# Reordering one gated-delta turn: which projections stand beside which step, and where ScalarE and VectorE take the next pair's convolutions and the old pair's gating

## The chip, the cores and the metric

The kernel runs on one core of a Trainium2 chip. The metric is the time of the whole program on the device in microseconds (us), lower is better. TensorE (PE) multiplies, VectorE (DVE), ScalarE (ACT) and GpSimd (POOL) do the rest, SyncE (SP) issues the loads. Each engine works through its own instructions in order and waits on semaphores for the others.

## The reference

Two blocks in a row over a sequence of 512 tokens of width 1024 in float32. The first has four SwiGLU feed-forward layers, a gated linear attention and a sparse attention. The second has a gated delta rule mixer and a forgetting attention, each behind a modulated norm. The change touches the gated delta mixer alone:

```python
def gated_delta_rule(q, k, v, g, beta):
    ...
    L = jnp.where(strict, jnp.einsum('bhncd,bhnsd->bhncs', kb, k) * decay, 0.0)
    T = lax.linalg.triangular_solve(eye + L, jnp.broadcast_to(eye, L.shape),
                                    left_side=True, lower=True, unit_diagonal=True)
    u = T @ vb
    w = T @ (kb * jnp.exp(g)[..., None])
    attn = jnp.einsum('bhncd,bhnsd->bhncs', q, k) * decay
    ...
    def step(state, inp):
        v_new = u_n - jnp.einsum('bhcd,bhde->bhce', w_n, state)
        o = (jnp.einsum('bhcd,bhde->bhce', q_n, state)
             + jnp.einsum('bhcs,bhse->bhce', a_n, v_new))
        state = state * gl_n[..., None, None] + jnp.einsum('bhcd,bhce->bhde', k_n, v_new)
        return state, o

def gdn_mixer(h, w_in, conv_w, A_log, dt_bias, norm_w, w_out):
    ...
    proj = h @ w_in
    ...
    qkv = jax.nn.silu(causal_depthwise_conv(qkv, conv_w))
    ...
    o = gated_delta_rule(q, k, v, g, beta)
    zg = jax.nn.silu(z.reshape(B, S, GDN_V_HEADS, GDN_HEAD_DIM).astype(jnp.float32))
    o = rmsnorm(o, norm_w) * zg
    return o.reshape(B, S, GDN_V_WIDTH).astype(h.dtype) @ w_out
```

Between the convolution and the rule q and k are normalised per head; each of the 8 q/k heads serves 2 of the 16 v heads.

## The kernel before, in words

Large products are made in split precision: a weight block of 128 x 1024 is loaded into `w_raw`, ScalarE rounds it to `w_hi` (L237), VectorE makes the rest `w_lo` (L243), and TensorE multiplies three times, hi by hi, hi by lo, lo by hi (L255). There are four raw and four split buffers, and splits run three blocks ahead of the products.

The gated-delta stage goes through 8 turns (`gdn_turns`): "first", six "mid" (a hardware loop of three rounds with two turns in its body), and "last". A turn j treats one q/k head with its two v heads. At the same time it projects q, k, v0, v1 of pair j+1 and z of pair j, and it makes the output tiles O0 to O7 of pair p = j-1. Each projection is cut into four units of six matmuls ("v12" is unit 2 of v1), and an output tile is one unit of six matmuls (L1749 to L1751). Results stand in a ring of four PSUM banks. The chain of a turn itself is made of small products: transposes "kt", "vt", the products "kk" and "qk", "sel" (L1816, picks rows for 15 elimination steps that VectorE makes on 16 x 16 blocks), then products of 64 x 64 (L1718), "f", "g", "c", "f2", "v", "y", "at", each of which combines blocks of the inverse, and then four chunks t of the recurrence: "ks" (L1848), "vn" (L1853), "o" (L1862, L1864), "ds" (L1867). At the end the squares of the output are summed (L1871).

What order stands where is written out by hand, engine by engine:

- TensorE: the table `GDN_BESIDE` names for each step the units that follow it. In a middle turn "v11 v12" stand beside "v", "v13 O0" beside "y", O1 beside "at", and "z11 z12 z13" beside "o3". Beside "at" also come the sums of the next pair's squares (`sums_next`, L1760), which read the buffers `G.sq`.
- ScalarE (`gdn_act`, `turn`): copies of small products ("fa", "fb", "c", "f2a", "y", "bt", "ct", all at L1996), splits (`GDN_SPLITS`), for the next pair the first tap of each convolution (`conv`, L1908), its silu (`silu`, L1913), the squares of q and k (`squares`, L1920) and copies of their sums (`sums`, L1925); for the old pair the high part of the gated output (`high`, L1989).
- VectorE (`gdn_dve`, `turn`): elimination steps, copies "ga", "gb", "f2b", "at", additions "va", "vb", the other three taps of each convolution (`conv`, L2112), for the old pair the product with the gate (`gated`, L2158), the low part (`low`, L2163) and the addition of output tiles into the residual (L2121).

`G.sq` is used twice: it holds the old pair's output until `low` has read it, and then the squares of the next pair. So `squares` waits for "lo_1". `silu(u)` waits until VectorE has done the last tap of convolution u (it frees the bank). TensorE's "at" waits for ScalarE's "bt", an output tile 0 for "lo_1".

## Time and profile before

| | |
|---|---|
| median of 3 runs | 2972.32 us (2971.85 to 2976.83) |
| the profiled execution | 2976.83 us, its span 2975.1 us |
| PE busy | 2822.0 us, 95% |
| DVE busy | 1664.2 us, 56% |
| ACT busy | 1249.0 us, 42% |
| POOL busy | 621.2 us, 21% |
| gated-delta turns (2025 to 2520) | about 71 us each |
| last chain, by engine | PE 77%, DVE 9%, ACT 5% |

The timeline gives one line for each instruction or run of equal ones: its start in us from the start of the span, its length, engine, line of the kernel, operation and tiles, the count (x), and in brackets the idle time of the engine just before it with what ended it. Matmuls overlap, so a row lasts longer than its distance to the next: 0.39 us long, 0.23 us apart for 512 columns at the full clock. Products of 64 x 64 and of 128 columns are made in several passes, so one step gives many counts.

### The profile page before, as it was taken

What the parts mean: (1) busy time and instruction counts of PE and PEld (TensorE: products, weight loads), DVE (VectorE), ACT (ScalarE), POOL (GpSimd) and SP (SyncE); (2) the same over time, 40 slices, a digit from 0 to 9 for tenths busy, and PEclk for the clock granted to TensorE, in tenths of its full rate; (3) what the DMA queues carried; (4) which work ended last, traced back from release to release, by engine and by line L of the source; (5) the groups of instructions that cost most, each with busy time, mean ns of one, the idle gap of its engine ahead of it and who ended that gap; (6) DMA issues with size and microseconds to landing.
All of it is one profiled execution on the core that took longest, in us unless ns stands there. A gap on an engine that the chain in (4) does not pass through costs nothing.

```text
span 2975.1 us, 41230 instructions
## 1 busy us (share of the span) xinstructions
PE 2822.0 (95%) x14333; PEld 2280.8 (77%) x14333; DVE 1664.2 (56%) x2500; ACT 1249.0 (42%) x1838; POOL 621.2 (21%) x594
## 2 busy tenths in 40 slices
PE   7999999999998999999898999979999999789998
PEld 5888877788887788886677788857888887567766
DVE  4444345454433664336845654265777777677773
ACT  4443242444423332233443322254555554456664
POOL 2000003100001440013424500214333333112221
PEclk8999998999999999999899999989999999899999
DMA  4333331233333553332114533312222222122211
GB/s 121 104 98 95 91 91 52 70 106 92 97 97 88 170 169 97 95 88 71 43 57 140 170 113 96 92 41 81 69 66 65 65 65 54 36 64 57 56 57 57
DMA packets 485304, 255.64 MB, mean 86 GB/s; under 512 B 18820, under 2 KB 479399, under 8 KB 485175
## 3 DMA queue, kind: packets, MB, share of 16 engines
q1 hardware_dynamic: 483856, 253.25, 29.8%
q8 instruction: 80, 1.31, 0.2%
q10 hardware_dynamic: 1318, 0.69, 0.1%
q14 instruction: 50, 0.40, 0.0%
HBM read 251.77 MB, written 2.13 MB: 85 GB/s over the span
## 4 chain that ended last, share of the span: by engine, by line
PE 77%; DVE 9%; ACT 5%; issue 4%; POOL 4%; ACTq 0%; DMA 0%; DVEq 0%; POOLq 0%; SPq 0%
PE bank L255 60%; PE bank L1718 2%; ACT w_hi L237 1%; POOL sumsq L585 1%; PE bank L2569 1%; POOL ada_sum L585 1%; DVE dsa_work L1456 1%; PE bank L1749 1%; PE bank L1816 1%; PE bank L1750 1%; PE bank L1751 1%; DVE prod L681 1%; DVE w_lo L243 1%; DVE small L1454 1%; DVE ada_hi L571 1%
## 5 line engine op out<-in xcount | busy, mean ns | idle before, releaser
L255 PE MATMUL bank<-x_hi,w_hi 128*128 128x512 f32 x2328 | 957.9, 411 | 10.0 <-DVE x_lo L484 3.5
L255 PE MATMUL bank<-x_hi,w_lo 128*128 128x512 f32 x2328 | 916.5, 394 | 0.0
L255 PE MATMUL bank<-x_lo,w_hi 128*128 128x512 f32 x2328 | 916.3, 394 | 0.0
L243 DVE TENSOR_TENSOR w_lo<-w_raw,w_hi 128x1024 fp32r<-128x1024 f32 x430 | 551.0, 1283 | 639.6 <-ACT w_hi L237 632.8
L237 ACT ACTIVATE w_hi<-w_raw 128x1024 fp32r<-128x1024 f32 x430 | 451.1, 1053 | 447.8 <-PE bank L255 414.2
L255 PEld LDWEIGHTS bank<-x_hi,w_hi 128*128 128x128 f32 x2328 | 442.8, 190 | 119.6 <-issue 19.9
L255 PEld LDWEIGHTS bank<-x_hi,w_lo 128*128 128x128 f32 x2328 | 442.1, 190 | 95.9
L255 PEld LDWEIGHTS bank<-x_lo,w_hi 128*128 128x128 f32 x2328 | 443.7, 191 | 91.9 <-issue 7.4
L400 POOL TENSOR_TENSOR sumsq<-sumsq,sq 128x512 f32<-128x512 f32 x54 | 91.6, 1697 | 1351.1 <-ACT sq L386 1349.7
L255 PE MATMUL bank<-h_hi,w_hi 128*128 128x512 f32 x832 | 323.9, 389 | 4.0 <-DVE h_lo L2675 2.4
L255 PE MATMUL bank<-h_hi,w_lo 128*128 128x512 f32 x832 | 323.7, 389 | 0.0
L255 PE MATMUL bank<-h_lo,w_hi 128*128 128x512 f32 x832 | 323.7, 389 | 0.0
L657 ACT ACTIVATE h_hi<-prod 128x512 f32 x88 | 55.6, 632 | 403.1 <-DVE prod L681 403.1
L255 PEld LDWEIGHTS bank<-h_hi,w_hi 128*128 128x128 f32 x832 | 156.2, 188 | 36.6 <-issue 4.3
L255 PEld LDWEIGHTS bank<-h_lo,w_hi 128*128 128x128 f32 x832 | 156.2, 188 | 32.6
L255 PEld LDWEIGHTS bank<-h_hi,w_lo 128*128 128x128 f32 x832 | 156.2, 188 | 32.3
L654 ACT ACTIVATE gate_s<-gate_s 128x512 f32<-128x512 f32 x88 | 55.6, 632 | 192.4 <-DVE gate_s L673 192.4
L678 DVE TENSOR_TENSOR prod<-bank,rstd 128x512 f32<-128x512 f32 x88 | 60.6, 689 | 101.8 <-PE bank L255 101.8
L684 DVE TENSOR_TENSOR h_lo<-prod,h_hi 128x512 f32 x88 | 62.2, 706 | 82.3 <-ACT h_hi L657 82.3
L585 POOL TENSOR_TENSOR sumsq<-sumsq,ada_hi 128x512 f32<-128x512 f32 x48 | 62.0, 1292 | 164.1 <-DVE ada_hi L571 164.1
L673 DVE TENSOR_TENSOR gate_s<-bank,rstd 128x512 f32<-128x512 f32 x88 | 60.4, 687 | 37.7 <-PE bank L255 37.7
L681 DVE TENSOR_TENSOR prod<-prod,gate_s 128x512 f32<-128x512 f32 x88 | 76.6, 871 | 4.5
(446 smaller groups left out, 3590.1 us busy)
## 6 DMA issues: line engine op xcount, KB each, us to landing
w_raw<-in_ffn_wi_dram SPq DMA_DIRECT2D x176, 512.0 KB, 3.8
w_raw<-in_ffn_wo_dram SPq DMA_DIRECT2D x64, 512.0 KB, 4.0
w_raw<-in_ada_w_dram SPq DMA_DIRECT2D x48, 512.0 KB, 4.9
w_raw<-in_a_w_in_dram SPq DMA_DIRECT2D x48, 512.0 KB, 4.0
w_raw<-in_b_w_in_dram SPq DMA_DIRECT2D x32, 512.0 KB, 4.1
w_raw<-in_ffn_wo_dram SPq DMA_DIRECT2D x32, 384.0 KB, 3.5
w_raw<-in_even_w_in_dram SPq DMA_DIRECT2D x16, 512.0 KB, 4.1
w_raw<-in_a_w_out_dram SPq DMA_DIRECT2D x16, 512.0 KB, 3.6
```

The lines of the kernel that those rows point to most:

```text
L237: act.activation(w_hi[b % SPLIT][:], w_raw[raw % RAW][:], ACT.Copy).then_inc(w_hi_done, 1)
L243: dve.tensor_tensor(w_lo[s][:], w_raw[raw_of(b) % RAW][:], w_hi[s][:].bitcast(F32), ALU.subtract).then_inc(w_lo_done, 1)
L255: mm = pe.matmul(out, lhs[:, w], rhs(kt), start=first and kk == 0 and m == 0, stop=last and kk == len(kts) - 1 and m == 2)
L400: pool.tensor_tensor(sumsq[:], sumsq[:], sq[k % 2][:], ALU.add).then_inc(sum_added, 1)
L585: pool.tensor_tensor(dst, x, y, ALU.add).then_inc(ada_added, 1)
L654: act.activation(gate_s[s][:], gate_s[s][:], ACT.Silu).then_inc(silu_done, 1)
L657: act.activation(h_hi[:, col(i * 2 + 2 * turn0 + s)], prod[s][:], ACT.Copy).then_inc(h_hi_done, 1)
L673: dve.tensor_tensor(gate_s[s][:], bank[(t0 + o) % BANKS][:], rstd[:], ALU.mult).then_inc(tile_free, 1)
L678: dve.tensor_tensor(prod[s][:], bank[(t0 + o + 1) % BANKS][:], rstd[:], ALU.mult).then_inc(tile_free, 1)
L681: dve.tensor_tensor(prod[s][:], prod[s][:], gate_s[s][:], ALU.mult).then_inc(prod_done, 1)
L684: dve.tensor_tensor(h_lo[:, h], prod[s][:], h_hi[:, h].bitcast(F32), ALU.subtract).then_inc(h_ready, 1)
L1718: mm = pe.matmul(out[:, c * INV_PART:(c + 1) * INV_PART], lhs(c), rhs(c), start=True, stop=True)
```

## The change

Nothing is computed otherwise; instructions change places on three engines.

TensorE, middle turn: "v12" moves from beside "v" to "y", "v13" from "y" to "at", O0 to beside "vn0" and each later output tile behind it by one or two steps, so that five units of z instead of three stand beside "o3". First and last turn are shifted likewise (in the last, nothing stands beside "v" and O0 stands beside "y").

ScalarE: silu of k moves from behind the copies "y" and "bt" to before the old pair's high parts, and so before these copies; the first tap of v0 from before the high parts to behind the squares; the first tap of v1 behind the copies of the sums.

VectorE: the gating of the old pair moves from before "ga" to behind the additions "va", "vb"; the low parts from before "va" to behind the copy "at" (in the last turn before it); the split "f" from behind the convolution of k to before it; the convolutions of v0 and v1 both behind the split "f2"; output tiles are added one or two steps later.

ScalarE in the middle turn before, from behind the copy of f2 (`gdn_W_0_231`); `gdn_kT_207` is k and `gdn_vT_234` is v0 of the next pair, `gdn_W_0_229` and `gdn_T` are the targets of copies "y" and "bt":

```order
L1996 ACTIVATE gdn_W_0_231<-bank 64x512
L1907 REGISTER_ALU
L1908 ISA
L1908 ACTIVATE gdn_vT_234<-bank,par 128x512
L1988 REGISTER_ALU
L1989 ACTIVATE gdn_o_hi_190<-gdn_sq_200 128x512
L1988 REGISTER_ALU
L1989 ACTIVATE gdn_o_hi_191<-gdn_sq_201 128x512
L237 ACTIVATE w_hi_58<-w_raw_54 128x1024
L1992 REGISTER_ALU
L1996 ACTIVATE gdn_W_0_229<-bank 64x512
L1996 ACTIVATE gdn_T<-bank 64x8x64
```

The same place of ScalarE now:

```order
L1994 ACTIVATE gdn_W_0_231<-bank 64x512
L236 REGISTER_ALU
L237 ACTIVATE w_hi_58<-w_raw_54 128x1024
L1912 REGISTER_ALU
L1913 ACTIVATE gdn_kT_207<-gdn_kT_207 128x512
L1986 REGISTER_ALU
L1987 ACTIVATE gdn_o_hi_190<-gdn_sq_200 128x512
L1986 REGISTER_ALU
L1987 ACTIVATE gdn_o_hi_191<-gdn_sq_201 128x512
L1990 REGISTER_ALU
L1994 ACTIVATE gdn_W_0_229<-bank 64x512
L1994 ACTIVATE gdn_T<-bank 64x8x64
```

The silu of k stands ahead of the two copies now, the tap of v0 has left this place, and the split has moved up.

VectorE in the middle turn before, from the split "vc" to the convolution of k; `gdn_W_1_232` is the target of the additions "va", "vb", and `gdn_sq` holds the old pair's gated output:

```order
L243 TENSOR_TENSOR w_lo_60<-w_raw_52,w_hi_56 128x1024
L2162 REGISTER_ALU
L2163 TENSOR_TENSOR gdn_o_lo_192<-gdn_sq_200,gdn_o_hi_190 128x512
L2162 REGISTER_ALU
L2163 TENSOR_TENSOR gdn_o_lo_193<-gdn_sq_201,gdn_o_hi_191 128x512
L2166 REGISTER_ALU x2
L2173 TENSOR_TENSOR gdn_W_1_232<-gdn_W_1_230,bank 64x512 x2
L2106 REGISTER_ALU
L2107 REGISTER_ALU
L2112 ISA
L2112 SCALAR_TENSOR_TENSOR gdn_kT_207<-bank,par,gdn_kT_207 128x511
```

The same place of VectorE now, from the additions on:

```order
L2173 TENSOR_TENSOR gdn_W_1_232<-gdn_W_1_230,bank 64x512 x2
L2156 REGISTER_ALU
L2157 REGISTER_ALU
L2158 TENSOR_TENSOR gdn_sq_200<-gdn_sq_200,gdn_zs_211 128x512
L2156 REGISTER_ALU
L2158 TENSOR_TENSOR gdn_sq_201<-gdn_sq_201,gdn_zs_212 128x512
L241 REGISTER_ALU
L243 TENSOR_TENSOR w_lo_61<-w_raw_53,w_hi_57 128x1024
L2107 REGISTER_ALU
L2112 ISA
L2112 SCALAR_TENSOR_TENSOR gdn_kT_207<-bank,par,gdn_kT_207 128x511
```

The gating and a split stand between the additions and the convolution of k. The low parts have moved on, to behind the copy "at", which writes `gdn_T`:

```order
L2112 SCALAR_TENSOR_TENSOR gdn_kT_207<-bank,par,gdn_kT_207 128x509
L2166 REGISTER_ALU
L2254 COPY gdn_T<-bank 64x8x64
L2162 REGISTER_ALU
L2163 TENSOR_TENSOR gdn_o_lo_192<-gdn_sq_200,gdn_o_hi_190 128x512
L2162 REGISTER_ALU
L2163 TENSOR_TENSOR gdn_o_lo_193<-gdn_sq_201,gdn_o_hi_191 128x512
L241 REGISTER_ALU
L243 TENSOR_TENSOR w_lo_62<-w_raw_54,w_hi_58 128x1024
```

Behind them now stand a split and the convolutions of v0 and v1.

The diff, with the table cut to the middle turn and without the order of semaphore names:

```diff
--- before.py
+++ after.py
@@ -1581,13 +1581,13 @@
 
 
         GDN_BESIDE = {
...
-            "mid": {"kt": "q0", "kk": "q1", "vt": "q2", "sel": "q3", "inv": "k0 k1 k2 k3 v00 v01 v02", "c": "v03", "f2": "v10", "v": "v11 v12", "y": "v13 O0",
-                    "at": "O1", "vn0": "O2", "ds0": "O3", "ks1": "O4", "vn1": "O5", "ds1": "O6", "ks2": "O7", "vn2": "z00", "ds2": "z01",
-                    "ks3": "z02", "vn3": "z03 z10", "o3": "z11 z12 z13"},
+            "mid": {"kt": "q0", "kk": "q1", "vt": "q2", "sel": "q3", "inv": "k0 k1 k2 k3 v00 v01 v02", "c": "v03", "f2": "v10", "v": "v11", "y": "v12",
+                    "at": "v13", "vn0": "O0", "ds0": "O1", "ks1": "O2", "vn1": "O3", "ds1": "O4", "ks2": "O5", "vn2": "O6", "ds2": "O7",
+                    "ks3": "z00", "vn3": "z01 z02", "o3": "z03 z10 z11 z12 z13"},
...
         GDN_SPLITS = {"first": {"start": "q", "vc": "k", "f": "v0", "f2": "v1", "at": "z0", "end": "z1"},
                       "mid": {"start": "q", "vc": "k", "f": "v0", "f2": "v1", "at": "Oa", "vn3": "Ob", "end": "z0 z1"},
...
@@ -1912,9 +1912,7 @@
                 act.wait_ge(*at.taken(GDN_CONV[u], i))
                 act.activation(x[:], x[:], ACT.Silu).then_inc(*N.act.done(f"cs{u}"))
 
-            def squares(j, odd, p=None):
-                if p is not None:
-                    act.wait_ge(*GdnOut.dve.after("lo_1", p))
+            def squares(j, odd):
                 for u in range(2):
                     act.wait_ge(*N.act.after(f"cs{u}", j))
                     act.activation(G.sq[u][:], gdn_conv(u, odd)[:], ACT.Square).then_inc(*N.act.done(f"sq_{'qk'[u]}"))
@@ -1955,12 +1953,12 @@
             act.wait_ge(*G.prep_dve.after("diff"))
             act.activation(G.kd, G.diff, ACT.Exp).then_inc(*s.done("kd"))
             silu(0, 0, front, 0)
+            silu(1, 0, front, 0)
             split(front, 0, "v0")
+            squares(0, 0)
             conv(2, 0, 0, front, 0)
-            silu(1, 0, front, 0)
-            squares(0, 0)
+            sums(0)
             conv(3, 0, 0, front, 0)
-            sums(0)
             split(front, 0, "v1")
             for u in (2, 3):
                 silu(u, 0, front, 0)
@@ -2028,18 +2026,19 @@
                     silu(0, i, at, odd)
                 pe("f2")
                 run("f2a", G.F2[a, :], first(0)[a], ACT.Copy)
+                splits("f2")
                 if more:
-                    conv(2, j + 1, i, at, odd)
+                    silu(1, i, at, odd)
                 if p is not None:
                     high(p)
-                splits("f2")
                 pe("y")
                 run("y", G.CY[b, :], first(0)[b], ACT.Copy)
                 run("bt", G.T[b, :, b], halves(first(1)[b]), ACT.Copy)
                 if more:
-                    silu(1, i, at, odd)
-                    squares(j + 1, odd, p)
-                    conv(3, j + 1, i, at, odd)
+                    if p is not None:
+                        act.wait_ge(*GdnOut.dve.after("lo_1", p))
+                    squares(j + 1, odd)
+                    conv(2, j + 1, i, at, odd)
                 else:
                     for h in range(2):
                         gate(h, at.through(f"z{h}", i), at.bank(f"z{h}"), (tile_free, BANKS + at.tile[f"z{h}"]))
@@ -2049,6 +2048,7 @@
                     sums(j + 1)
                 splits("at")
                 if more:
+                    conv(3, j + 1, i, at, odd)
                     silu(2, i, at, odd)
                 for t in range(TT):
                     for h in range(2):
@@ -2231,8 +2231,6 @@
                     if p is not None:
                         dve.wait_ge(*gdn_gate(at, i, 1)[3])
                     conv(0, j + 1, i, at, odd)
-                if p is not None:
-                    gated(p, [gdn_gate(at, i, h)[3] for h in range(2)])
                 pe("g")
                 for n, r, src in (("ga", a, second(0)), ("gb", b, second(1))):
                     dve.tensor_copy(G.m[r, :], src[r]).then_inc(*done(n))
@@ -2241,23 +2239,26 @@
                 pe("f2")
                 dve.tensor_copy(G.F2[b, :], first(1)[b]).then_inc(*done("f2b"))
                 splits("vc")
-                if p is not None:
-                    low(p)
                 pe("v")
                 own("hb")
                 for n, r, src in (("va", a, second(0)), ("vb", b, second(1))):
                     tt(n, G.V[r, :], G.V1[r, :], src[r], ALU.add)
+                if p is not None:
+                    gated(p, [gdn_gate(at, i, h)[3] for h in range(2)])
+                splits("f")
                 if more:
                     conv(1, j + 1, i, at, odd)
-                splits("f")
+                else:
+                    low(p)
+                pe("at")
+                dve.tensor_copy(G.T[a, :, a], halves(first(0)[a])).then_inc(*done("at"))
+                if more and p is not None:
+                    low(p)
+                splits("f2")
                 if more:
                     conv(2, j + 1, i, at, odd)
-                pe("at")
-                dve.tensor_copy(G.T[a, :, a], halves(first(0)[a])).then_inc(*done("at"))
-                if more:
                     conv(3, j + 1, i, at, odd)
-                splits("f2")
-                if not more and p is not None:
+                elif p is not None:
                     dve.wait_ge(tile_free, BANKS + at.tile["O0"])
                     outs(0, 1)
                 splits("at")
@@ -2269,7 +2270,7 @@
                             dve.scalar_tensor_tensor(G.W1[h][:, 3 * P:4 * P], first(h)[:, 3 * P:4 * P], G.neg_eg[:, bass.ds((j * 2 + h) * TT + t, 1)],
                                                      G.v_tok[h][:, x], ALU.mult, ALU.add).then_inc(*done(f"r{t}_{h}"))
                     if more:
-                        outs(*((0,), (2,), (5,), (7,))[t])
+                        outs(*((), (1, 2), (4,), (7,))[t])
                     else:
                         outs(*((2,), (3,), (5,), (7,))[t])
                     for h in range(2):
@@ -2283,7 +2284,7 @@
                         else:
                             dve.tensor_copy(S, add).then_inc(*done(f"s{t}_{h}"))
                     if more:
-                        outs(*((1,), (3, 4), (6,), ())[t])
+                        outs(*((0,), (3,), (5, 6), ())[t])
                     else:
                         outs(*((), (4,), (6,), ())[t])
                     splits(f"vn{t}")
```

## Rows read from the trace of the kernel before

**Rows 1.** The page, part 1: busy time, share of the span and count of instructions of each engine.

```profile
PE 2822.0 (95%) x14333; PEld 2280.8 (77%) x14333; DVE 1664.2 (56%) x2500; ACT 1249.0 (42%) x1838; POOL 621.2 (21%) x594
```

**Rows 2.** Stretches: length; busy us (instructions) of PE, PEld, DVE, ACT, POOL; TensorE's granted clock; DMA; GB/s.

```profile
2172.00:2243.00 71.00, 69.51 (x518) 56.95 (x517) 51.40 (x94) 37.20 (x61) 22.84 (x17) 1.00 0.24 69
```

**Rows 3.** Timeline of TensorE in a middle turn.

```profile
2176.90 1.15 PE L1718 MATMUL bank<-gdn_W,gdn_W 64*64 64x64 f32 x32
2177.97 0.50 PE L255 MATMUL bank<-x_hi,w_hi 128*128 128x512 f32 x1
...
2180.92 0.27 PE L1718 MATMUL bank<-gdn_W,gdn_W 64*64 64x64 f32 x1
...
2184.95 0.27 PE L1718 MATMUL bank<-gdn_P,gdn_W 64*64 64x64 f32 x1
...
2187.52 1.88 PE L1760 MATMUL bank<-gdn_sq,ones 128*128 128x512 f32 x4
2189.24 0.61 PE L1853 MATMUL bank<-gdn_v_tok,gdn_T 128*128 128x128 f32 x4
...
2190.84 0.40 PE L1751 MATMUL bank<-gdn_o_hi,w_lo 128*128 128x512 f32 x1
2191.81 0.49 PE L1864 MATMUL bank<-gdn_attnT,gdn_W 128*128 128x128 f32 x2 [0.57 <-ACT gdn_W L1996]
```

**Rows 4.** Waits of the stage, 2000 to 2600: us in total, times, longest.

```profile
PE bank L1816 <- DVE gdn_blocks L2195: 6.1, 6, 2.0
```

**Rows 5.** Timeline of VectorE in the same turn.

```profile
2171.47 1.28 DVE L2158 TENSOR_TENSOR gdn_sq<-gdn_sq,gdn_zs 128x512 f32<-128x512 f32 x2
...
2177.29 1.29 DVE L2163 TENSOR_TENSOR gdn_o_lo<-gdn_sq,gdn_o_hi 128x512 fp32r<-128x512 f32 x2
2178.61 1.40 DVE L2173 TENSOR_TENSOR gdn_W<-gdn_W,bank 64x512 f32<-64x512 f32 x2
2180.05 2.54 DVE L2112 SCALAR_TENSOR_TENSOR gdn_kT<-bank,par,gdn_kT 128x511 f32<-128x511 f32 x3
2182.50 1.30 DVE L243 TENSOR_TENSOR w_lo<-w_raw,w_hi 128x1024 fp32r<-128x1024 f32 x1
2183.72 2.52 DVE L2112 SCALAR_TENSOR_TENSOR gdn_vT<-bank,par,gdn_vT 128x511 f32<-128x511 f32 x3
2186.16 0.67 DVE L2256 COPY gdn_T<-bank 64x512 f32<-64x512 f32 x1
```

**Rows 6.** Timeline of ScalarE in the same turn.

```profile
2176.47 1.14 ACT L1989 ACTIVATE gdn_o_hi<-gdn_sq 128x512 fp32r<-128x512 f32 x2
2177.51 1.05 ACT L237 ACTIVATE w_hi<-w_raw 128x1024 fp32r<-128x1024 f32 x1
2182.11 0.60 ACT L1996 ACTIVATE gdn_W<-bank 64x512 f32<-64x512 f32 x1 [3.55 <-PE bank L1718]
2182.61 0.58 ACT L1996 ACTIVATE gdn_T<-bank 64x512 f32<-64x512 f32 x1
2183.22 0.63 ACT L1913 ACTIVATE gdn_kT<-gdn_kT 128x512 f32<-128x512 f32 x1
2183.75 0.62 ACT L1920 ACTIVATE gdn_sq<-gdn_qT 128x512 f32<-128x512 f32 x1
...
2189.93 1.05 ACT L237 ACTIVATE w_hi<-w_raw 128x1024 fp32r<-128x1024 f32 x1
```

**Rows 7.** Timeline of TensorE, the first middle turn's start and the last turn.

```profile
2076.57 1.15 PE L1708 MATMUL bank<-gdn_kT 128*128 128x128 f32 x8 [2.47 <-ACT gdn_W L1976]
...
2079.86 0.63 PE L255 MATMUL bank<-x_hi,w_lo 128*128 128x512 f32 x1
...
2514.68 2.03 PE L1816 MATMUL bank<-gdn_blocks,sumsq 128*128 128x128 f32 x8 [2.02 <-DVE gdn_blocks L2195]
...
2559.64 1.98 PE L1871 MATMUL bank<-gdn_W,ones 128*128 128x512 f32 x4 [0.76 <-ACT gdn_W L1996]
```

**Rows 8.** Stretches of TensorE: length, busy us (instructions), granted clock, DMA, GB/s.

```profile
2076.00:2080.00 4.00, 3.43 (x19) 0.73 0.50 135
```

## What the change was predicted to do

> **What bounds the kernel now.** I read the page's engine line first, then the table of stretches for the gated-delta stage, then the timelines of TensorE, VectorE and ScalarE through one middle turn, then the waits. TensorE is busy 95% of the span [rows 1], and in a middle turn of this stage 69.51 us of 71 at full clock [rows 2]. So a turn can gain only what TensorE still waits, and it loses every microsecond that another engine comes late. Two waits of a middle turn are marked. The product of L1864 starts 0.97 us after the last matmul before it, where 0.23 is the pace, so it waits 0.74 us for ScalarE. The product of L1816 waits for VectorE's reductions, six times in the stage, 6.1 us in all [rows 3, 4]. A third wait is unmarked: f2 is about 0.17 us late because VectorE gates the old pair's rows before it copies "gb".
>
> Between "v" and "at" the three engines run close together. "v" starts at 2176.90, two units (12 matmuls, 1.37 us a unit) cover VectorE's additions, "y" starts at 2180.92, two more units cover ScalarE's copies "y" and "bt", and "at" starts at 2184.95 [rows 3]. ScalarE is idle for 3.55 us before copy "y", so it is early. VectorE's rows from 2177.29 on carry no idle time, so it is the one that runs without a rest there [rows 5, 6].
>
> **The change, part by part.** All times are for the middle turn shown. Up to f2 nothing moves but the gating (1.20 us from one instruction to the next), so f2 and "v" start about 0.17 us earlier, "v" at 2176.73.
>
> *v to y.* VectorE's additions start at 2177.95 and end at 2179.35 (1.40) [rows 5]. One unit instead of two stands beside them on TensorE, so "y" could start at 2179.41 and starts at about 2179.50. Wait: 0.1.
>
> *y to at, the main term.* "at" needs ScalarE's copy "bt". With one unit beside "y" TensorE is ready at 2182.18. But ScalarE's silu of k now stands ahead of copies "y" and "bt", and it waits for VectorE's convolution of k. VectorE does, from 2177.95 on: additions 1.44, gating 1.20, weight split 1.22, convolution 2.45 (distances from start to start in [rows 5]; neither the gating nor the split stood between them before). The convolution ends at 2184.26. Then ScalarE: silu 0.53, the two high parts 1.04, "y" 0.50, "bt" 0.58 [rows 6], which ends at 2186.98; "at" starts at 2187.1. Wait: 4.9 us. ScalarE's early split of the weights costs nothing, it fits into the idle time.
>
> *at to sums.* The low parts now stand behind VectorE's copy of "at". That copy comes 1.21 us after "at" starts, 2188.3, and takes 0.63; the low parts end 1.32 later, 2190.25. Only then may ScalarE overwrite the two buffers with squares, 0.53 for the first. The sums of L1760 start at about 2191.0. TensorE, with one unit beside "at", is ready 2.57 us after "at" (2184.95 to 2187.52 in [rows 3]), at 2189.67. Wait: 1.35.
>
> *sums to vn0's copies.* The sums take 1.72, so ScalarE's second copy of them can start at 2192.9. Behind it stand a split (1.05 long, 0.95 to the next), now also the first tap of v1's convolution (0.6), the silu of v0 (0.5) and then the copies that L1864 needs, which it sees 0.4 after their start [rows 3, 6]. L1864 starts at 2195.87; TensorE, after the sums, vn0 (0.36) and one unit, is ready at 2194.43. Wait: 1.45, where 0.74 stood.
>
> *The first state copy.* VectorE still owes after the low parts: split 1.22, convolution of v0 2.45 (from 2192.1, when ScalarE has laid its first tap), that of v1 2.5 (from 2195.05, likewise), split 1.22. Its state copies start at 2198.7, and L1848 at 2199.0. TensorE is ready at 2198.2. Wait: 0.85. From here on the turn runs as before; output tiles come one or two steps later, and each bank is freed in time. The splits that moved also release SyncE's loads (a raw buffer is free after its low split); the last of them comes about 8 us later, and its buffer is read again only in the next turn, so I cost that at nothing; a load that came late would show as ScalarE waiting for DMA.
>
> *The turn's end.* Five units of z stand after the last L1864 instead of three. ScalarE, GpSimd and VectorE, whose chain leads from there to L1816, get 2.74 us more cover. But the sums of L1871 come later too, and with them ScalarE's roots and VectorE's split, so VectorE's reductions come about 1.5 later. Net cover is 1.2, more than the 0.8 to 1.0 that is waited. This wait goes: -0.98 in five middle turns. What is late next there is f, which has 0.6 in hand.
>
> A middle turn thus waits 0.1 + 4.9 + 1.35 + 1.45 + 0.85 = 8.65 and loses 0.17 + 0.74 of old waits: +7.74. Six of them: +46.4; L1816 in five of them: -4.9.
>
> *First turn.* No old pair, so no gating, no high and low parts: 4.9 less 1.20, 1.04 and some tenths is 2.5; the sums wait for nothing, the later two waits stay. +4.0.
>
> *Last turn.* The first output tile waits for the low parts, which come 1.20 + 1.22 + 1.32 = 3.7 after VectorE's additions while TensorE has only "y" to do: 2.7 waited, and "y" itself waits 0.9 more, since nothing stands beside "v". Against it stand the 2.02 that L1816 waits there (of which its later reductions, 1.2 as above, give only 1.5 back) and 0.76 at the last sums [rows 7]. Net 2.7 + 0.9 - 1.5 - 0.8 = +1.3. *Before the first turn* the squares pass one tap (-0.5 at best), but the tap of v1 now waits for the copies of the sums, and VectorE and the roots follow it by an instruction's length: +0.6, the later end.
>
> Sum without the clock: 46.4 - 4.9 + 4.0 + 1.3 + 0.6 = +47.4 us.
>
> *The clock.* After a wait of 2.47 us before L1708 the matmuls of the next microseconds took 0.63 instead of 0.39, and the granted clock of that stretch is 0.73, so both levels, 2.4 and 1.2 GHz, lie in it; after the wait of 2.02, eight products of L1816 took 2.03 instead of 1.13, and the waits under 1 us were followed by no such row [rows 3, 7, 8]. Each fall cost about 1.6 us of dense work. A wait of 4.9 will do the same in each turn. But behind "at" TensorE waits again for the others, so part of the slow work is hidden: bounds 0 and 3.3 (two falls), I take 0.8, half of one fall, near the lower end because the row nearest to it has dense work behind it and this place has not. Six times: +5.
> The Trainium skill ("TensorE: Matmul & The Clock Gate", "HAM oscillation — how this bites in real kernels") says that idle gaps between bursts of matmuls put the array back to half rate at every gap. It speaks against this change; by it each turn pays a fall, by the rows under 1 us no turn paid one before. The trace agrees with both halves.
>
> The profiled execution took 2976.83 us with a span of 2975.1; the median of the three runs is 2972.32, the low one 2971.85, so the profiled one is the slowest by 4.5. The sum goes on the median: 2972.3 + 52.4 = 3024.7, say 3025.
>
> **The rivals.** (A) *The clock falls deeper.* Two falls in each middle turn, for "at" and for L1864, with little hidden: 47.4 + 6 x 3.3 = +67, 3039. For it: the wait is twice as long as any that the rows show inside the loop, and three others follow within 12 us. Against: those others are under 1.5. The page named above would give this, if every gap counted.
> (B) *The later waits melt.* VectorE and ScalarE catch up while TensorE waits for "at", so only that wait counts: 6 x (4.9 + 0.1) - 6 x 0.17 - 4.9 + 2.5 + 1.3 + 0.6 = +28.5, 3001. Against it: VectorE's debt behind "at" (low parts, two splits, two convolutions, 8.7 us) can't be worked off earlier, since it stands behind the copy of "at" in its order.
> (C) *Faster.* Only the turns' ends and f2 count: -4.9, -1.5 - 0.8 in the last turn, -6 x 0.17, together -8.2, 2964. It needs the convolution of k to end 4.9 us earlier than I have it, before 2179.4; from that point silu, high parts and copies are hidden under the unit of "y". For it: the wait at L1816 is real and its cover is. Against: additions, gating, split and convolution are 6.3 us in one row on one engine, behind "v".
> (D) *No change:* the middle wait is about 1 us and eats the gain of the end. It needs 3.9 us of slack that no row shows.
>
> **How the numbers follow.** My forecast 0.62, (A) 0.18, (B) 0.13, (C) 0.04, (D) 0.03. The forecast's own range is 3014 to 3034: clock 0 to one whole fall in each turn, and 0.7 us for a turn's waits. With (A) whole and (B) as far as 3007, the range is 3006 to 3044. A measurement of this kernel tells 0.2% (6 us) from no change. Slower by more than that: forecast, A and B, 0.93; within: D, 0.03; faster: C, 0.04.
>
> **What would show it.** In the changed kernel's timeline of a middle turn: ScalarE's silu of gdn_kT starts right behind VectorE's third convolution step, with ScalarE idle 4 to 7 us before it; L1718's last group ("at") shows TensorE idle near 4.9 us, for ScalarE; L1760 waits for a square, 1 to 1.5 us; L1864 waits 1.2 to 1.7; the wait of L1816 is gone in the middle turns; rows of 0.63 us instead of 0.39 stand behind "at"; the stretch that a turn fills grows from 71 or 72 us to 78 to 80. I am wrong if TensorE's idle time before "at" is under 2 us, if the later waits are nearly nothing (B), or if L1816 still waits.

## The result, and the profile after

The changed kernel takes 3046.21 us (median of 4 runs, 3043.9 to 3049.34); the kernel before takes 2972.09 us beside it. The ratio is 1.0247, interval 1.0229 to 1.0265: **slower**, as forecast, but by 74 us where the forecast's sum said 52.4, and 2 us above the end of the range (3044). The profiled execution took 3047.69 us with a span of 3045.9, 70.8 us more than the span before; the accounts below are made on these two spans.

The first line of the page, the stretch of 71 us that holds most of the middle turn, and the 5 us behind "at" (columns as in [rows 2]):

```profile
PE 2839.6 (93%) x14333; PEld 2291.7 (75%) x14333; DVE 1675.4 (55%) x2500; ACT 1250.6 (41%) x1838; POOL 626.9 (21%) x594
```

```profile
2184.00:2255.00 71.00, 61.74 (x473) 49.52 (x472) 43.83 (x60) 33.82 (x56) 23.71 (x17) 0.93 0.25 68
2204.50:2209.50 5.00, 4.95 (x39) 3.88 (x40) 2.95 (x4) 0.94 (x2) 0.00 (x0) 0.50 0.01 3
```

The same number of instructions on every engine; TensorE is busy 61.74 us of 71 where it was 69.51 [rows 1, 2], and the granted clock of the last line is 0.50, the 1.2 GHz level, over the whole 5 us. The waits of TensorE in the stage, 2000 to 2680 (line waited at and what ended the wait; us in total, times, longest):

```profile
PE bank L1718 <- ACT gdn_T L1994: 45.5, 7, 7.2
PE bank L1730 <- POOL gdn_kT L2324: 10.1, 1, 10.1
...
PE bank L1864 <- ACT gdn_W L1994: 8.2, 7, 1.3
PE bank L1848 <- DVE gdn_W L2285: 4.6, 8, 0.7
PE bank L1718 <- DVE gdn_W L2173: 2.8, 7, 1.6
```

The wait before "at" stands at the top, with 7.1 to 7.2 us in each middle turn and 2.6 in the first. L1816, which led to 6.1 us before [rows 4], is gone from the list. TensorE's timeline of a middle turn, to be laid beside [rows 3]:

```profile
2194.68 0.24 PE L1718 MATMUL bank<-gdn_W,gdn_W 64*64 64x64 f32 x1 [0.23 <-DVE gdn_W L2173]
...
2204.55 0.34 PE L1718 MATMUL bank<-gdn_P,gdn_W 64*64 64x64 f32 x1 [7.13 <-ACT gdn_T L1994]
...
2207.04 0.63 PE L255 MATMUL bank<-x_lo,w_hi 128*128 128x512 f32 x1
...
2209.25 2.42 PE L1760 MATMUL bank<-gdn_sq,ones 128*128 128x512 f32 x4
2211.51 0.61 PE L1853 MATMUL bank<-gdn_v_tok,gdn_T 128*128 128x128 f32 x4
...
2214.66 0.49 PE L1864 MATMUL bank<-gdn_attnT,gdn_W 128*128 128x128 f32 x2 [1.15 <-ACT gdn_W L1994]
```

and VectorE's, ScalarE's and GpSimd's of the same place, to be laid beside [rows 5, 6]:

```profile
2193.01 1.40 DVE L2173 TENSOR_TENSOR gdn_W<-gdn_W,bank 64x512 f32<-64x512 f32 x2 [0.81 <-PE bank L1718]
2194.44 2.37 DVE L2158 TENSOR_TENSOR gdn_sq<-gdn_sq,gdn_zs 128x512 f32<-128x512 f32 x2
2196.74 2.30 DVE L243 TENSOR_TENSOR w_lo<-w_raw,w_hi 128x1024 fp32r<-128x1024 f32 x1
2199.07 2.54 DVE L2112 SCALAR_TENSOR_TENSOR gdn_kT<-bank,par,gdn_kT 128x511 f32<-128x511 f32 x3
2206.55 0.68 DVE L2254 COPY gdn_T<-bank 64x512 f32<-64x512 f32 x1 [4.95 <-PE bank L1718]
...
2201.63 0.63 ACT L1913 ACTIVATE gdn_kT<-gdn_kT 128x512 f32<-128x512 f32 x1 [9.84 <-DVE gdn_kT L2112]
...
2203.82 0.58 ACT L1994 ACTIVATE gdn_T<-bank 64x512 f32<-64x512 f32 x1
...
2194.59 3.36 POOL L2317 TENSOR_TENSOR gdn_dec<-gdn_gb,not_above 128x512 f32<-128x512 f32 x2 [22.58 <-DVE gdn_W L2173]
2197.91 3.02 POOL L2320 TENSOR_TENSOR gdn_dec<-gdn_dec,gdn_cols 128x512 f32<-128x512 f32 x2
```

The path of the forecast is there link by link: additions, gating, split, convolution of k, then ScalarE's silu of k at the moment the convolution ends, the high parts, the two copies, "at". But two links are longer than they were: the gating 2.37 instead of 1.28 and the split 2.30 instead of 1.30 [rows 5]. They lie exactly beside GpSimd's L2317 and L2320. GpSimd is released by VectorE's additions ("vb"), which stood ahead of the convolution before and stand ahead of the gating and the split now.

Where the 70.8 us of span are, by the starts of "f" (32 small products of L1718) in both traces: from the first middle turn on, five periods take 71.64 us each before (2098.11 to 2456.31) and 82.17 after (2102.18 to 2513.04), and the sixth, up to the last turn's "f", 71.40 and 80.55. That is 5 x 10.53 + 9.15 = 61.8 us. The last turn gives 4.85 from "f" to L1871 (31.93 to 36.78), the first 4.7 from "f" to "f" (65.95 to 70.67), and the front of the stage, from the products of L1777 to the first "f", 0.5. Ahead of that, where the kernels are the same, the changed one is 1.1 early in its trace (L1777 at 1982.30 instead of 1983.43). Together 70.7. Below, "us a turn" is always the mean of such periods without the sixth. Where a run is set against the changed kernel in us of the whole time, it goes by the two ratios, since each stands against its own runs of the kernel before.

### The profile page after: what moved, and what is told of

Read it like the earlier page. It is cut to its first block, busy times and chain, and to the rows that moved or that the text cites. A ratio compares the mean times of both kernels' runs of the same rounds, so it can differ in the third digit from the quotient of the medians.

```text
span 3045.9 us, 41218 instructions
## 1 busy us (share of the span) xinstructions
PE 2839.6 (93%) x14333; PEld 2291.7 (75%) x14333; DVE 1675.4 (55%) x2500; ACT 1250.6 (41%) x1838; POOL 626.9 (21%) x594
## 3 DMA queue, kind: packets, MB, share of 16 engines
q8 instruction: 80, 1.31, 0.2%
HBM read 251.77 MB, written 2.13 MB: 83 GB/s over the span
## 4 chain that ended last, share of the span: by engine, by line
PE 75%; DVE 11%; ACT 5%; issue 4%; POOL 3%; ACTq 0%; DMA 0%; DVEq 0%; POOLq 0%; SPq 0%
PE bank L255 59%; PE bank L1718 2%; DVE w_lo L243 1%; ACT w_hi L237 1%; POOL sumsq L585 1%; PE bank L2570 1%; POOL ada_sum L585 1%; DVE dsa_work L1456 1%; DVE prod L681 1%; DVE small L1454 1%; PE bank L1816 1%; PE bank L1749 1%; PE bank L1751 1%; PE bank L1750 1%; DVE ada_hi L571 1%
## 5 line engine op out<-in xcount | busy, mean ns | idle before, releaser
L243 DVE TENSOR_TENSOR w_lo<-w_raw,w_hi 128x1024 fp32r<-128x1024 f32 x430 | 553.0, 1287 | 646.0 <-ACT w_hi L237 639.2
```

The costliest lines, as they stand in the source:

```text
L243: dve.tensor_tensor(w_lo[s][:], w_raw[raw_of(b) % RAW][:], w_hi[s][:].bitcast(F32), ALU.subtract).then_inc(w_lo_done, 1)
```

## The experiments

Three theories of the 21 us that the forecast missed. **Contention:** VectorE's gating and split, both with two operands in SBUF, are held up by GpSimd's two pairs of products, some 2.3 us a turn. **Clock:** the half clock behind the long wait costs more than the 0.8 us counted. **Order:** the chain is longer than counted through its order alone (table, place of the silu, place of the low parts). They exclude one another only in size, so each was taken out by itself, and at the end the first two together.

### GpSimd released later

```diff
-                    dve("PT" if p is None else "vb")
+                    dve("PT" if p is None else "s0_1")
```

> The changed kernel, but GpSimd begins its additions for the next pair's decay behind VectorE's second state copy of chunk 0 instead of behind the addition vb. Theory 1 (VectorE's gating and split run at half speed because GpSimd's tensor operations run beside them): the gating takes 1.28 us again (2.37 in the changed kernel) and the split beside it 1.23 to 1.30 (2.30), TensorE's wait before at falls from 7.1 to about 4.9, six middle turns give 6 x 2.2 = 13 us: 3033. Rival (the excess over the forecast is the clock's): both stay near 2.3 and the time stays within 3 us of 3046.

Measured 3039.52 us, ratio 1.0208 (1.0189 to 1.0226), 79.88 us a turn. VectorE in the same place:

```profile
2191.81 1.29 DVE L2158 TENSOR_TENSOR gdn_sq<-gdn_sq,gdn_zs 128x512 f32<-128x512 f32 x2
2193.02 1.22 DVE L243 TENSOR_TENSOR w_lo<-w_raw,w_hi 128x1024 fp32r<-128x1024 f32 x1
```

and the first line of TensorE's waits, 2000 to 2600:

```profile
PE bank L1718 <- ACT gdn_T L1994: 32.6, 7, 5.0
```

Gating and split are back at the durations of [rows 5] with VectorE's own order unchanged, and the wait falls from 7.2 to 5.0, next to the 4.9 forecast. A turn saves 82.17 - 79.88 = 2.29 us, and VectorE's busy time is 1662.6 us instead of 1675.4. Contention is shown.

### GpSimd released after the copy of "at"

The same line, with "at" in place of "s0_1".

> The changed kernel, but GpSimd begins behind VectorE's copy of at. Theory 1: gating 1.28 and split 1.30 as above, the wait before at 4.9, but now the low parts (1.28) and the split behind them (1.21) run beside GpSimd and take 2.3 to 2.4 each; the low parts lie on the path to the sums, the split is hidden by VectorE's wait for the tap of v0. Net 2.2 - 1.1 = 1.1 a turn, 3039. Rival (something else slows gating and split in their new place): they stay at 2.3, the low parts at 1.28, 3046.

Measured 3038.03 us, 1.0209 (1.019 to 1.0228), 79.75 us a turn. The time is near the 3039 expected, but not for its reason. Which engine is held up was expected wrongly:

```profile
2200.96 1.28 DVE L2163 TENSOR_TENSOR gdn_o_lo<-gdn_sq,gdn_o_hi 128x512 fp32r<-128x512 f32 x2
2202.16 1.21 DVE L243 TENSOR_TENSOR w_lo<-w_raw,w_hi 128x1024 fp32r<-128x1024 f32 x1
...
2201.21 4.52 POOL L2317 TENSOR_TENSOR gdn_dec<-gdn_gb,not_above 128x512 f32<-128x512 f32 x2 [33.26 <-DVE gdn_T L2254]
```

VectorE's low parts and split keep their 1.28 and 1.21, and GpSimd's pair takes 4.52 us, where it took 2.54 with GpSimd released after the state copy. VectorE was at it first, and GpSimd's first product came through only when VectorE's row of such instructions was over. Nothing waits for GpSimd there, so it costs nothing.

### The kernel before, GpSimd released earlier

```diff
-                    dve("PT" if p is None else "vb")
+                    dve("PT")
```

> The kernel before with one edit on GpSimd: its part of each turn for the next pair (L2317, L2320 and on) is released after VectorE's copy PT in every turn instead of after the additions in the later turns, so it starts some 10 us earlier and runs beside VectorE's gating (L2158). Theory (VectorE's products of two SBUF operands and GpSimd's delay each other when they run side by side, and nothing in the changed kernel's order is needed for that): the rows of L2158 or L243 that fall beside GpSimd's L2317 and L2320 take 2.2 to 2.4 us instead of 1.3, rows that read PSUM (L2112, L2173) stay at 2.54 and 1.40; TensorE loses at most 1.2 us a turn at f2 or v: ratio 1.000 to 1.003. Rival (the slow gating of the changed kernel comes from its own operands or place in the order): all rows of L2158 and L243 stay at 1.3 us.

Measured 2983.2 us beside 2978.09 for before, ratio 1.0016 (1.0006 to 1.0025); 72.61 us a turn. VectorE's gating in the old order, GpSimd beside it, and TensorE's "g", which VectorE's next copies release:

```profile
2172.51 2.35 DVE L2158 TENSOR_TENSOR gdn_sq<-gdn_sq,gdn_zs 128x512 f32<-128x512 f32 x2
...
2172.83 2.93 POOL L2319 TENSOR_TENSOR gdn_dec<-gdn_dec,gdn_cols 128x512 f32<-128x512 f32 x2
...
2176.33 1.15 PE L1718 MATMUL bank<-gdn_W,gdn_W 64*64 64x64 f32 x32 [1.16 <-DVE gdn_W L2238]
```

The contention can be made at will without any of the change's moves: 2.35 us for the gating, and 1.0 us a turn on TensorE.

### The silu of k back behind the copies

ScalarE's `silu(1)` back from ahead of the high parts to behind "bt"; all else as in the changed kernel:

```diff
-                if more:
-                    silu(1, i, at, odd)
                 if p is not None:
                     high(p)
                 pe("y")
...
                 if more:
+                    silu(1, i, at, odd)
                     if p is not None:
                         act.wait_ge(*GdnOut.dve.after("lo_1", p))
```

> The changed kernel with ScalarE's silu of k put back behind the copies y and bt, all else as changed. If the wait before at comes from that silu: at waits about 1.8 (for the high parts, which wait for the gating) instead of 7.1, the sums wait about 2.4 for the squares, later waits as they are; 5.1 us less a turn and less of the slow clock, 5.6 x 6 and 2 in the first turn, 36 us: 3010. If the high parts or the low parts were the cause, the wait before at would stay above 5 and the time above 3035.

Measured 3022.36 us, 1.0158 (1.0141 to 1.0175), 78.19 us a turn: about 26 us less than the changed kernel where 36 were expected.

```profile
2189.91 0.24 PE L1718 MATMUL bank<-gdn_P,gdn_W 64*64 64x64 f32 x1 [1.34 <-ACT gdn_T L1994]
2195.39 3.68 PE L1760 MATMUL bank<-gdn_sq,ones 128*128 128x512 f32 x4 [2.75 <-ACT gdn_sq L1918]
```

The wait of 7.1 shrinks to 1.34, which is what the blocked gating does through the high parts. But the sums now wait 2.75 us: the convolution of k starts 6.1 us behind the additions, as late as ever, VectorE's copy of "at" and the low parts stand behind it in its row, and the squares wait for the low parts. The sums then take 3.68 against 1.88, at half clock. Taking the silu out moves the wait one step on.

### The gating back ahead of "ga"

```diff
+                if p is not None:
+                    gated(p, [gdn_gate(at, i, h)[3] for h in range(2)])
                 pe("g")
...
-                if p is not None:
-                    gated(p, [gdn_gate(at, i, h)[3] for h in range(2)])
                 splits("f")
```

> The changed kernel with VectorE's gating put back ahead of the copies ga and gb, where GpSimd is idle. Theory 1: gating 1.28 there, and the way from the additions to the convolution of k loses 2.3 us, six times, with 0.17 lost at f2: -13, 3033. If the gating costs what my forecast gave it (1.20): -6, 3040.

Measured 3028.0 us, 1.0169 (1.0152 to 1.0186), 78.37 us a turn: 23 us less where 13 were expected. Only the gating's place and its own delay had been counted. But the split behind it was not held up either:

```profile
2192.33 1.23 DVE L243 TENSOR_TENSOR w_lo<-w_raw,w_hi 128x1024 fp32r<-128x1024 f32 x1
...
2192.48 3.46 POOL L2317 TENSOR_TENSOR gdn_dec<-gdn_gb,not_above 128x512 f32<-128x512 f32 x2 [22.59 <-DVE gdn_W L2173]
```

The split starts 0.15 us ahead of GpSimd, so GpSimd is the one that stands (3.46 for the pair instead of 2.54). The gating's move thus cost 3.8 us a turn (82.17 - 78.37), of which its own 1.2 and the 2.3 of contention make 3.5.

### Both back

The two edits above together.

> The changed kernel with two edits undone together: ScalarE's silu of k behind the copies y and bt, and VectorE's gating before the copy ga. What remains is the table, the low parts behind the copy of 'at', the later taps and the split ahead of the convolution of k. Theory (the parts of the prediction's sum hold one by one): 'at' waits for nothing, the sums wait about 1, L1864 1.3 and L1848 0.85 us, L1816 for nothing: 72.5 to 74 us a middle turn, ratio 1.003 to 1.008. If the two single undoings simply added (-26 and -23 us) it would be -49 us against the changed kernel, ratio 1.0085. Rival (the low parts behind 'at' cost as much as the silu ahead of it, the wait only moves to the sums): 75 us or more a turn, ratio 1.012 or above.

Measured 2997.51 us, 1.0066 (1.0051 to 1.0082), 73.71 us a turn. TensorE's marked waits in a middle turn:

```profile
2190.12 1.99 PE L1760 MATMUL bank<-gdn_sq,ones 128*128 128x512 f32 x4 [1.15 <-ACT gdn_sq L1918]
...
2195.09 0.49 PE L1864 MATMUL bank<-gdn_attnT,gdn_W 128*128 128x128 f32 x2 [1.15 <-ACT gdn_W L1994]
...
2198.32 0.71 PE L1848 MATMUL bank<-gdn_W,gdn_kT 128*128 128x128 f32 x4 [0.70 <-DVE gdn_W L2284]
```

"At" waits for nothing, and the three later waits of the prediction stand alone with nearly the sizes it gave them (a mark is about 0.17 smaller than a wait as the prediction counts it: 1.15 marked is its 1.32). These two moves were about three quarters of the loss (1.0247 to 1.0066).

### The table alone, and the silu alone

The kernel before with the changed table and nothing else:

> The kernel before with one part of the change: TensorE's table of units beside the steps (all three kinds of turn); ScalarE's and VectorE's orders stay as before. Theory (VectorE's order is the cause, the table only takes cover away that the old order did not need): 'y' waits 0.5 us for VectorE's additions, 'at' waits for nothing (ScalarE's copy bt came 2.3 us before 'at' was ready), L1864 and L1848 wait 0.7 to 1.5 together since TensorE comes two units earlier to VectorE's state copies, L1816 no longer waits (-0.98). Sum about +1 us a middle turn: ratio 1.000 to 1.006 of before, no falls of the clock over 1 us. Rival (the table alone makes at least half of the loss): a wait of 2 us or more before 'at' or the sums in each turn, 4 us or more a turn, ratio 1.010 or above.

Measured 2979.68 us, ratio 1.0004 (0.9995 to 1.0014), 71.82 us a turn. Waits 2000 to 2600, first lines without those of the stage's front:

```profile
PE bank L1718 <- DVE gdn_W L2173: 5.4, 7, 1.6
PE bank L1864 <- ACT gdn_W L1996: 4.1, 7, 0.7
```

No wait before "at", none at L1816. What "y" waits, 0.62 in a middle turn, and what is lost up to L1848 eat what the end of the turn gives back.

The kernel before with the silu of k directly ahead of the copies:

```diff
                 splits("f2")
+                if more:
+                    silu(1, i, at, odd)
                 pe("y")
...
                 if more:
-                    silu(1, i, at, odd)
                     squares(j + 1, odd, p)
```

> The kernel before with one edit on ScalarE: the silu of k stands ahead of the copies y and bt, directly before them. Theory (the silu only passes on VectorE's lateness: the convolution of k ends at 2182.5 in the old order, so silu, y and bt end by 2184.1 and TensorE is ready at 2184.95): no wait before 'at', 71.6 us a turn, ratio 0.999 to 1.001. Rival (the silu ahead of the copies is enough by itself to make the wait): 1 us or more before 'at' in each turn, ratio 1.002 or above.

Measured 2975.67 us, 0.9996 (0.9986 to 1.0005), 71.64 us a turn. Neither move costs anything by itself that the time can tell. The silu makes a wait before "at" only where VectorE's convolution is late, and so does the missing unit beside "y" only where "bt" is.

### TensorE kept busy through the wait

The changed kernel with products that add no result, into output tile 0's bank:

```diff
                 beside("y")
+                if at.kind == "mid":
+                    pe.wait_ge(*at.free("O0", i))
+                    s = at.block["v1"] % SPLIT
+                    for _ in range(29):
+                        pe.matmul(at.bank("O0")[:], w_hi[s][:, 0:P], x_hi[:, 0:T], start=True, stop=True)
                 act("bt")
```

> The changed kernel, and 29 more matmuls (128x512) in each middle turn, between the unit beside 'y' and the wait for bt, into output tile 0's bank, which is free then and is written anew later: they add no result, only keep TensorE busy through the wait of 7.2 us before 'at' (29 x 0.23 = 6.7 us). Theory (part of the loss is the half clock behind this wait): L1718's pieces at 'at' back from 0.31 to 0.22 us, the sums of L1760 back from 2.42 to about 1.9, starts of the other engines unchanged up to 'at', -1.3 us a middle turn, about -8 us, ratio to before about 1.022 instead of 1.0247. Rival (the half clock lies beside other waits and costs nothing, all is VectorE's and ScalarE's lateness): the same time as the changed kernel within 2 us, since the sums wait longer for the squares by as much.

Measured 3043.4 us beside 2978.09, 1.0218 (1.0197 to 1.0238), 81.19 us a turn, 0.98 less than the changed kernel. The intervals of the two ratios overlap a little; the rows do not:

```profile
2199.00 0.24 PE L1718 MATMUL bank<-gdn_P,gdn_W 64*64 64x64 f32 x1 [0.62 <-ACT gdn_T L1999]
...
2202.88 1.98 PE L1760 MATMUL bank<-gdn_sq,ones 128*128 128x512 f32 x4 [1.15 <-ACT gdn_sq L1923]
2204.70 0.61 PE L1858 MATMUL bank<-gdn_v_tok,gdn_T 128*128 128x128 f32 x4
...
2200.19 0.68 DVE L2259 COPY gdn_T<-bank 64x512 f32<-64x512 f32 x1 [4.14 <-PE bank L1718]
```

From "at" to the sums it is 3.88 us instead of 4.70, from the sums to vn0 1.82 instead of 2.26 (over the five periods, "at" to L1864 is 1.13 shorter in the mean). VectorE's copy follows "at" by 1.19 instead of 2.00. So the half clock is not hidden behind the wait for the squares: it makes the products of "at" themselves longer, VectorE's copy hangs on their end, and the low parts, the squares and the sums hang on that copy. The sums no longer show a wait in the changed kernel (its last product before them starts at 2208.74 and takes 0.43 to the next, so it is ready at 2209.17, and they start at 2209.25), because the slow clock has filled it, not because it is gone.

### Both additions out

GpSimd released at "s0_1", and 20 such products instead of 29.

> The changed kernel with both suspected additions taken out together: GpSimd's part of a turn is released after VectorE's first state copy (as in the run with GpSimd late), and 20 more matmuls (128x512, 4.6 us, into output tile 0's bank, which is written anew later; they add no result) stand in the wait before 'at' of each middle turn. What remains is what the prediction's sum counted: waits from the order of the instructions alone. Theory (2.2 us a turn are VectorE blocked by GpSimd, 1.0 to 1.3 the half clock, the rest the order): a middle turn takes 78.5 to 79 us where the changed kernel takes 81.9, gating 1.3, split 1.2, sums 1.98 and their wait about 1.1; ratio 1.017 to 1.019. Rival (the two overlap, since a shorter wait makes the slow stretch shorter too): no better than GpSimd late alone, 79.8 us and 1.0208.

Measured 3029.85 us, 1.0187 (1.017 to 1.0204), 78.83 us a turn, 3.34 less than the changed kernel. The two savings measured apart, 2.29 and 0.98, add up to 3.27. What is left is a turn 7.2 us longer than before, where the prediction has 7.74 - 0.98 = 6.8 without its clock term. So the third theory, order, is left with 0.4.

### A version that beats both

The kernel before with one unit moved: O0 beside "at" and not "y", each later tile one place on, four units of z beside "o3".

```diff
-            ... "v": "v11 v12", "y": "v13 O0", "at": "O1", "vn0": "O2", ... "o3": "z11 z12 z13"},
+            ... "v": "v11 v12", "y": "v13", "at": "O0", "vn0": "O1", ... "o3": "z10 z11 z12 z13"},
```

> The kernel before with the middle turn's table shifted by one unit only, behind 'y' (O0 moves from beside 'y' to beside 'at', each later tile by one place, and four units of z stand beside o3 instead of three); other engines as before. Theory (the good half of the change is the fourth unit at the turn's end, and 'y' had a unit more cover than bt needs): the wait at L1816 (0.98 us in five turns) is gone, 'at' starts 1.37 us earlier and waits for nothing, L1864's 0.74 grows to at most 1.4: -2 to -6 us, ratio 0.998 to 0.9993. Rival (VectorE's state copies set the start of ks1, so each unit taken from in front of them comes back as a wait): +1 us or more a turn, ratio 1.001 to 1.003.

Measured 2971.31 us beside 2978.09, ratio 0.9977 (0.9968 to 0.9987), 70.58 us a turn. The same with the silu of v0 behind vn0's copies:

> The kernel before with the middle turn's table shifted by one unit behind 'y' (as in the run with four units at the end, which gave 70.5 us a turn) and ScalarE's silu of v0 behind vn0's copies instead of ahead of them. Theory (L1864 waits for ScalarE's copies, and the silu of 0.5 us stands in front of them): L1864's idle 0.57 falls to 0.1, a middle turn takes 70.0 us, about -10 us in all: ratio 0.9960 to 0.9972. Rival (VectorE's state copies then end last, or another engine waits for v0): the turn stays at 70.5 us and the ratio at 0.9977.

Measured 2969.63 beside 2976.52, 0.9978 (0.9968 to 0.9989), where 0.9960 to 0.9972 was expected. The wait at L1864 is gone (0.57 before [rows 3]) and the turn is 70.22 us, but the time can't be told from that of the first version. From the sums to L1864 a turn is 0.52 shorter than in the first version, and 0.14 of it comes back at L1848:

```profile
2187.11 0.49 PE L1864 MATMUL bank<-gdn_attnT,gdn_W 128*128 128x128 f32 x2
...
2189.26 0.40 PE L1751 MATMUL bank<-gdn_o_hi,w_lo 128*128 128x512 f32 x1
2189.62 0.71 PE L1848 MATMUL bank<-gdn_W,gdn_kT 128*128 128x128 f32 x4
```

L1848 starts 0.36 behind the last product where 0.23 is the pace, for VectorE's state copy. So both theories of that run hold in part: the turn falls, if not to 70.0, and VectorE's state copy comes last at L1848. Both versions beat the kernel before by about 0.2%, with intervals that end below 1.

## Why the prediction came short

Direction, place and the main wait's mechanism were right; the size was off by 21 us of 74. (On the two spans, of which the one before is of the slowest run, it is 18.4 of 70.8: 17.0 in the six middle turns, 2.05 in the last, 0.7 in the first, less 1.1 from ahead of the stage.) By its own steps:

- *v to y, 0.1:* nearly right. "Y" starts with 0.23 marked.
- *y to at, 4.9: this step failed, by its size.* It measured 7.2. The silu did start the moment the convolution ended, and ScalarE's part took what was said. What was mis-sized is VectorE's part, "gating 1.20, weight split 1.22": they took 2.30 and 2.33 (starts 2194.44, 2196.74, 2199.07). Both durations had been read from rows where GpSimd was idle or where VectorE was first, and put down at a place where GpSimd's release had been left standing right ahead of them. 2.3 us a turn, some 13 in all (the two ratios differ by 0.0039, 11.6 us); the run with GpSimd late shows that 4.9 would have been 5.0.
- *The sign of it was in the trace of before.* GpSimd's two instructions of L2319 beside VectorE's split [rows 5], by their durations (min, median, max in ns):

```profile
L2319 POOL TENSOR_TENSOR gdn_dec<-gdn_dec,gdn_cols x2: 1035/1532/2029, 2182.7 to 2184.7; 128x512 f32<-128x512 f32 x2
```

  The first took 2029 ns and the second, alone, 1035: GpSimd stood still for the rest of the split. The prediction counted the splits and SyncE's loads but never laid GpSimd's timeline beside VectorE's.

  The Trainium skill ("SBUF — State Buffer", "Who interferes with whom") says that a VectorE instruction with two inputs in SBUF contends with a GpSimd instruction that reads SBUF, calls the shared port pair an exclusive lock, and says that issue order decides who blocks. The traces agree: instructions that take one of their tensors from PSUM, or their only one, are not longer beside GpSimd (the convolution of k, L2112, 2.54 beside it in the changed kernel; in the kernel before with GpSimd early the convolution of q 2.50 and the copies of L2238 1.40, where the trace of before has 2.49 and 1.40), and those with two in SBUF are (L2158, L243), by the rest of GpSimd's instruction. An estimate from GpSimd's rows in the kernel before, two products of L2316 of 1.28 each, one of them for the gating and one for the split, would have put the two at 2.48 and 2.50 instead of 1.20 and 1.22.
- *at to sums, 1.35:* at full clock it measured 1.31 (3.88 - 2.57, in the run with TensorE kept busy). In the changed kernel it is 4.70 - 2.57 = 2.13, with the clock in it.
- *The clock, 0.8 a turn:* too small. 0.82 from "at" to the sums and 0.44 on the sums, 1.26 in these rows; 0.98 over a whole turn with TensorE kept busy. The reason given for a small term ("part of the slow work is hidden") failed: the chain itself runs through the slow products.
- *L1864, 1.45:* the wait is 1.32. *L1848, 0.85:* it is 0.84. *L1816, -0.98 in five turns:* gone in each, and nothing took its place. All three right. (In the last turn, where the wait at L1816 is gone too, "f" waits 2.56 for VectorE instead of 0.94.)
- *First turn +4.0, front +0.6:* measured 4.7 and 0.5. The first turn has a slow stretch too, which the clock term did not count. "At" there, in the changed kernel and with GpSimd late:

```profile
2046.73 0.34 PE L1718 MATMUL bank<-gdn_P,gdn_W 64*64 64x64 f32 x1 [2.63 <-ACT gdn_T L1994]
2047.80 0.24 PE L1718 MATMUL bank<-gdn_P,gdn_W 64*64 64x64 f32 x1 [2.62 <-ACT gdn_T L1994]
```

  In the first its products are slow (0.34) and it is 3.89 to the sums, in the second they are not (0.24) and it is 2.58, and the first turn is 3.45 longer than before.
- *Last turn +2.8 from "f" on* (its +1.3 without the -1.5 for L1816, which falls ahead of "f"): measured 4.85. Its "v", "y" and output tile 0:

```profile
2599.27 1.97 PE L1718 MATMUL bank<-gdn_W,gdn_W 64*64 64x64 f32 x32 [0.90 <-DVE gdn_W L2240]
2602.83 0.33 PE L1718 MATMUL bank<-gdn_W,gdn_W 64*64 64x64 f32 x1 [1.59 <-DVE gdn_W L2173]
...
2606.45 0.77 PE L1749 MATMUL bank<-gdn_o_hi,w_hi 128*128 128x512 f32 x1 [1.64 <-issue]
```

  The waits of 1.59 and 1.64 stand for the 0.9 and 2.7 forecast: 3.2 marked where 3.6 was said, but not in these shares. The rest, about 2 us, is by these rows the half clock, which had been counted for the middle turns only. It is there from "v" on (1.97 for its 32 products, 1.15 before), ahead of both waits. No run took this one apart.

In sum, a turn was put at 7.6 (7.74 - 0.98 + 0.8) and came out at 10.5. Of the 2.9 between them 2.3 are GpSimd's, 0.2 the clock's beyond its 0.8 (0.5 by the rows alone), and 0.4 are left in the run with both out, 7.2 against 6.8. There four links are each a little longer than the prediction had them: "v" to "y" 2.95 for 2.77, "y" to "at" 7.72 for 7.6, the sums to L1864 4.97 for 4.87, from there to L1848 3.24 for 3.13. Rival A had the amount nearly right (3039) for the wrong reason: one fall in each turn, as forecast, not two. B is out (all the later waits are there), C and D as well.

**Open:** which engine gets through. GpSimd slipped in between the two gating instructions in the changed kernel, but not between the two low parts or ahead of the split behind them. All of these stand back to back in VectorE's queue, and no run tells why.

## What to carry to other kernels

A duration holds for the place where it was read. When an instruction with two SBUF operands moves on VectorE, lay GpSimd's timeline beside both its old and its new place, and look at what releases GpSimd: here that release was left ahead of the moved work, and nearly the whole difference to the forecast's main term is this (the wait is 7.2 us with it and 5.0 without, against 4.9). The half clock behind a wait is not hidden by the next wait when the chain of the other engines hangs on the first products behind it: here it cost 1.0 to 1.3 us a turn where 0.8 had been counted. And a move that costs nothing alone can be dear beside another: table and silu each measured no change, and the table by one unit less than here even gained 0.2%.

## What the runs showed of the hardware

- VectorE and GpSimd hold each other up by whole instructions, not by a share. In the changed kernel the gating pair has one of 0.69 and one of 1.76 us, as GpSimd's first product goes in between:

```profile
L2158 DVE TENSOR_TENSOR gdn_sq<-gdn_sq,gdn_zs x2: 691/1226/1760, 2194.4 to 2195.1; 128x512 f32<-128x512 f32 x2
L2317 POOL TENSOR_TENSOR gdn_dec<-gdn_gb,not_above x2: 1675/1702/1728, 2194.6 to 2196.2; 128x512 f32<-128x512 f32 x2
```

  Columns: min, median and max in ns, first and last start in us. GpSimd's first takes 1.28 alone; here it starts at 2194.59 and takes 0.39 more, which ends at 2194.98, shortly before VectorE's first does (2195.13); VectorE's second then stands until GpSimd's first is over at 2196.3.
- The trace counts the time that an engine stands in this way as busy. So DVE's busy time rose (1664.2 [rows 1] to 1675.4 us) with the same 2500 instructions, and no wait was marked; with GpSimd late it was 1662.6. The busy share of an engine doesn't show such a loss, the durations of one form of instruction do.
- A wait of 7.1 us put TensorE at 0.50 of its clock for the 5 us behind it; the waits of 1.15 us at L1864 were followed by rows of 0.39 us, at full clock. In between it is not the wait alone that decides: behind the same wait of 2.6 us the first turn's "at" was slow in the changed kernel and not in the run with GpSimd late.
